# Modulation products of a two-block transformer kernel: fp32 in four column groups, most of them placed in the first block's attentions

## What is computed

```python
mod = (silu_c @ lp["w_mod"] + lp["b_mod"])[:, None, :]
sh1, sc1, gt1, sh2, sc2, gt2 = jnp.split(mod, 6, axis=-1)
h = modulate(x, lp["g_norm1"], sh1, sc1)      # rms_norm(x, g) * (1 + sc1) + sh1
x = x + gt1 * merge_branches(...)
x = x + gt2 * conv_ffn(modulate(x, lp["g_norm2"], sh2, sc2), lp)
```

## Time and profile before

| | |
|---|---|
| median of 3 runs | 2862.47 us (2861.6 to 2864.29) |
| profiled execution | 2865.59 us, span 2863.8 us |
| PE busy | 2627.9 us, 92% of the span |
| DVE, ACT, POOL busy | 61%, 51%, 21% |
| DMA | 450.55 MB, mean 157 GB/s |
| issues of `raw<-in_w_mod` | 192 of 256 KB |

### The profile page before, as it was taken

How to read it: one execution, slowest core, us unless ns; L and a number is a source line. 1 busy time by engine, 2 the same in 40 slices (tenths; PEclk the granted TensorE clock), 3 DMA queues, 4 the chain that set the end, 5 groups by cost and what they waited for, 6 DMA issues and landing times.

```text
span 2863.8 us, 48110 instructions
## 1 busy us (share of the span) xinstructions
PE 2627.9 (92%) x17790; PEld 2304.9 (80%) x17790; DVE 1748.5 (61%) x2491; ACT 1465.8 (51%) x2248; POOL 604.5 (21%) x432
## 2 busy tenths in 40 slices
PE   5769999999899999699999999999799999979998
PEld 2538978988877898588589979978699789857996
DVE  6564756776675776657667756553566554455455
ACT  5454554665445575354446645444454454446444
POOL 0001202332111233221032323212032033011311
PEclk9788999999999999899999999999899999999999
DMA  9684515655541565354135565656156546633663
GB/s 302 207 273 129 164 53 149 182 177 163 156 127 39 154 190 181 92 160 148 38 120 169 182 191 178 195 166 194 48 155 202 172 149 191 187 114 89 191 194 123
DMA packets 332946, 450.55 MB, mean 157 GB/s; under 512 B 28192, under 2 KB 207392, under 8 KB 332768
## 3 DMA queue, kind: packets, MB, share of 16 engines
q1 hardware_dynamic: 332400, 446.58, 50.4%
q0 software_dynamic: 368, 1.57, 0.2%
HBM read 446.99 MB, written 1.05 MB: 156 GB/s over the span
## 4 chain that ended last, share of the span: by engine, by line
PE 82%; DVE 7%; DMA 4%; ACT 4%; issue 2%; POOL 1%; SPq 1%; DVEq 0%; ACTq 0%; POOLq 0%
PE S L818 26%; PE S L809 21%; PE G L818 14%; PE G L809 9%; DMA raw<-in_w_mod 4%; PE TB L868 3%; PE S L897 2%; DVE wlo L603 2%; ACT whi L598 2%; PE G L935 1%; ACT pp L1191 1%; PE TB L776 1%; PE G L920 1%; PE S L959 1%; PE G L959 1%
## 5 line engine op out<-in xcount | busy, mean ns | idle before, releaser
L603 DVE TENSOR_TENSOR wlo<-raw,whi 128x1024 fp32r<-128x1024 f32 x723 | 946.4, 1318 | 779.0 <-ACT whi L598 773.2
L598 ACT CAST whi<-raw 128x1024 fp32r<-128x1024 f32 x872 | 904.5, 1049 | 838.5 <-PE S L809 261.6
L818 PE MATMUL S<-hhi,whi 128*128 128x256 f32 x1952 | 547.6, 281 | 4.0 <-issue 2.4
L818 PE MATMUL S<-hhi,wlo 128*128 128x256 f32 x1952 | 547.7, 281 | 0.0
L818 PE MATMUL S<-hlo,whi 128*128 128x256 f32 x1952 | 546.6, 280 | 0.0
L603 POOL TENSOR_TENSOR wlo<-raw,whi 128x1024 fp32r<-128x1024 f32 x149 | 362.1, 2430 | 758.6 <-ACT whi L598 757.9
L818 PEld LDWEIGHTS S<-hhi,whi 128*128 128x128 f32 x1952 | 367.3, 188 | 5.6 <-issue 5.1
L818 PEld LDWEIGHTS S<-hlo,whi 128*128 128x128 f32 x1952 | 368.6, 189 | 0.2
L818 PEld LDWEIGHTS S<-hhi,wlo 128*128 128x128 f32 x1952 | 368.0, 189 | 0.0
L818 PE MATMUL G<-hhi,whi 128*128 128x256 f32 x1088 | 305.3, 281 | 2.9 <-issue 2.7
L818 PE MATMUL G<-hhi,wlo 128*128 128x256 f32 x1088 | 305.0, 280 | 0.0
(11 more groups left out here) (340 smaller groups left out, 4543.1 us busy)
## 6 DMA issues: line engine op xcount, KB each, us to landing
raw<-in_ffn_wi SPq DMA_DIRECT2D x352, 256.0 KB, 3.5
raw<-in_w_up SPq DMA_DIRECT2D x264, 256.0 KB, 3.5
raw<-in_w_mod SPq DMA_DIRECT2D x192, 256.0 KB, 3.8
raw<-in_w_in SPq DMA_DIRECT2D x192, 256.0 KB, 3.2
raw<-in_ffn_wo SPq DMA_DIRECT2D x160, 256.0 KB, 3.4
raw<-in_w_down SPq DMA_DIRECT2D x120, 256.0 KB, 3.4
raw<-in_a_wqkv SPq DMA_DIRECT2D x72, 256.0 KB, 2.9
raw<-in_w_o SPq DMA_DIRECT2D x48, 256.0 KB, 3.2
```

What stands on the lines that cost most here:

```text
L598: act.copy(whi[:, n0 % SPLIT], raw[:, n0 % RAW]).then_inc(hi_done, 1)
L603: eng.tensor_tensor(wlo[:, n0 % SPLIT], raw[:, n0 % RAW], whi[:, n0 % SPLIT].bitcast(F32), ALU.subtract)\
L818: mm = pe.matmul(out_[:, m * T:(m + 1) * T], w, x, start=first and c == 0 and m == 0 and z == 0, stop=last and c == kc - 1 and z == len(te ...
```

## The change

The stages `mod` and `modcols` of both layers go. One stage `mod` with four units (shift 1 and scale 1 of layer 0) stands at the start. The other 20 units stand inside the first block's attentions: 8 in A (layer 0, pieces 4 to 11), 4 in B (layer 1, pieces 0 to 3), 8 in C (layer 1, pieces 4 to 11), at the steps of the table `MODS`. There is no split: the weights are loaded as fp32 into `modw`, two buffers of a whole unit (2 MB each, 8 DMAs of 256 KB), which lie over `whi` and `wlo`. A unit is 8 matmuls of 512 columns (2 chunks x 4 column groups of 32), all into the bank `G0[1]`; `silz` holds 30 columns of zeros and then the two rows, and its window moves by two columns a unit, so each unit's result comes to rows of its own. One copy (DVE), four small matmuls with `fold` and one addition give all columns of a stage.

Since `G0[1]` is taken, the pairs of these attentions all use `G0[0]`, and their copy and multiplication move to the head of the even steps. Since `modw` covers `whi` and `wlo`, the last unit of `gates` splits nothing ahead; the three slots of `br` are split at the end of the attention instead. SP loads the first four raw slots of `br` before the units, waits until `gates` is multiplied, and then loads the units, each when the one two before it is used. At the start SP loads two units, then the constants and the context, then the other two, then the latents.

```diff
+MODS = {(0, CTX): (0, 4, 8, (0, 1, 4, 8, 11, 14, 17, 19)), (0, LAT): (1, 0, 4, (0, 2, 4, 6)),
+        (1, LAT): (1, 4, 8, (0, 2, 4, 6, 8, 10, 12, 14))}
+MOD_SLOTS, MOD_W = 4, 32
...
-    for l in range(DEPTH):
-        gemm("mod", 6 * D // SN, KD, l=l)
-        add("modcols", u=1, x=1, l=l)
+    add("mod", u=1, mod=(0, 0, 4, ()))
...
+        def value_bank(st, p):
+            return G0[0] if st.mod else G0[p % 2]
+        def lead_steps(st, n):
+            return (n + 1, n + 2, n + 3) if max(st.mod[3]) < n else (n + 4,) * LEAD
...
+            def load_mod(st, i):
+                g = mod_base[st] + i
+                wait_count(sp, mod_used, g - 1)
+                src = mod_source(st, i)
+                for z in range(MOD_SLOTS):
+                    for c in range(SK):
+                        sp.dma_start(modw[:, g % 2 * MOD_SLOTS + z, c, :], src[:, z * SK + c, :]).then_inc(mod_full[g % 2], 16)
...
+                if st.kind == "attn" and st.mod:
+                    ahead = STAGES[STAGES.index(st) + 2]
+                    for k in range(RAW // len(slot_shapes(ahead.kc))):
+                        load_unit(ahead, k, k, 0)
+                    sp.wait_ge(bank_done[1], st.n)
+                    for i in range(st.mod[2]):
+                        load_mod(st, i)
...
+            def mod_unit(st, i):
+                g = mod_base[st] + i
+                pe.wait_ge(mod_full[g % 2], 16 * MOD_SLOTS * SK * (g // 2 + 1))
+                for c in range(SK):
+                    for z in range(MOD_SLOTS):
+                        mm = pe.matmul(G0[1][z * MOD_W:(z + 1) * MOD_W - 2 * i, :], silz[:, z * SK + c, 2 * i:MOD_W],
+                                       modw[:, g % 2 * MOD_SLOTS + z, c, :], start=i == 0 and c == 0,
+                                       stop=i == st.mod[2] - 1 and c == SK - 1, skip_group_check=True)
+                mm.then_inc(mod_used, 1)
+            def mod_fold(st):
+                pe.wait_ge(mod_copied, mods.index(st) + 1)
...
                 for s in range(n + VALUE_LAG):
                     if s < n:
                         scores(s)
                     if TURN_LAG <= s < n + TURN_LAG:
                         turn(s - TURN_LAG)
+                    if st.mod and s in st.mod[3]:
+                        mod_unit(st, st.mod[3].index(s))
                     if s >= VALUE_LAG:
                         values(s - VALUE_LAG)
+                if st.mod:
+                    mod_fold(st)
...
+                        if st.mod and s >= VALUE_LAG + 2 and s % 2 == 0:
+                            weighted((s - VALUE_LAG - 2) // 2)
...
+                        if st.mod and s == n + VALUE_LAG - 1:
+                            mod_copy(st)
+                        if st.mod:
+                            for h in [h for h, step_ in enumerate(lead_steps(st, n)) if step_ == s]:
+                                lo_part(dve, st.n + h, st.n + h, None, None)
+                    if st.mod:
+                        mod_columns(st, 1 + st.pad)
+                        dve.wait_ge(mod_done, mods.index(st) + 1)
+                    dve.wait_ge(pair_free, pair0 + len(pairs_))
+                    dve.tensor_copy(mx[:, 0:1], mhalf[:, 0:1]).then_inc(bank_free[0], 1 + st.pad)
```

More of the change, by code:

```diff
@@ L257, in loop_shape @@
     per = len(slot_shapes(st.kc))
-    if st.kind not in ("mod", "gates", "up", "qkv") or st.units < 2 * PAIRS:
+    if st.kind not in ("gates", "up", "qkv") or st.units < 2 * PAIRS:
         return 0, 0, st.units
@@ L550, in modulation, with mod_source, mods_needed, follows_mod @@
             return amul[:, st.l, w, c, st.s:st.s + 1], modT[:, st.l, 3 * w * KD + c, st.s:st.s + 1]
+        mods = [st for st in STAGES if st.mod]
+        mod_base = {st: sum(z.mod[2] for z in mods[:n]) for n, st in enumerate(mods)}
+        def mod_source(st, i):
+            l, first, count, _ = st.mod
+            c0 = (first + count - 1 - i) * SN
+            return dram["w_mod"][l].rearrange("(c p) n -> p c n", p=P)[:, :, c0:c0 + SN]
+        def mods_needed(st):
+            return 2 * st.l + int(st.which)
+        def follows_mod(st):
+            return st.kind == "gates" and st.part == 1
+        def value_bank(st, p):
+            return G0[0] if st.mod else G0[p % 2]
+        def lead_steps(st, n):
+            return (n + 1, n + 2, n + 3) if max(st.mod[3]) < n else (n + 4,) * LEAD
         def lo_by_pool(st, n0):
@@ L765, in _ @@
         def _(pe):
+            def mod_unit(st, i):
[9 more added lines that the diff above has]
+                pe.wait_ge(mod_copied, mods.index(st) + 1)
+                n = 2 * st.mod[2]
+                for q in range(SN // P):
+                    mm = pe.matmul(G0[1][:, q * n:(q + 1) * n], modsum[:, q * P:(q + 1) * P], fold[:, MOD_W // 2 - n:],
+                                   start=True, stop=True, skip_group_check=True)
+                mm.then_inc(mod_folded, 1)
             def turn_rows(st, n):
@@ L1098, in _ @@
             act.wait_ge(ld_cols, 16)
-            act.activation(silc[:, :, :], col("c", 0, 2 * KD).rearrange("p (k s) -> p k s", s=2), ACT.Silu).then_inc(silc_done, 1)
-            act.wait_ge(silc_done, 1)
-            act.copy(silr[:, :, 0:2], silc[:, :, :]).then_inc(silc_done, 1)
+            act.activation(silz[:, :, MOD_W - 2:], col("c", 0, 2 * KD).rearrange("p (k s) -> p k s", s=2), ACT.Silu)\
+               .then_inc(silz_done, 1)
+            act.wait_ge(ld_ctx, 16)
+            for t in range(NT):
+                row_squares(norms[0], t)
+            act.wait_ge(mod_used, mods[0].mod[2])
             for n in range(LEAD):
@@ L1117, in _ @@
                 if st.kind == "norm" and not inside(st):
-                    if st.which == "1":
+                    if st.which == "1" and st is not norms[0]:
                         for t in range(NT):
```

256 lines of the change are left out of this document (142 added, 114 removed).

## The result

The changed kernel took 2711.89 us in the median of 4 runs (2710.83 to 2713.81), the kernel before 2862.63 (2861.6 to 2864.29) on the same chip: ratio 0.9474, 95% interval 0.9462 to 0.9486. It is faster by 5.3%, as forecast; the forecast of 2702 us was 9.9 us too low. The profiled execution of after took 2710.83 us (span 2709.0), so against the profiled 2865.59 of before the change is worth -154.8 us where the sum said -160.7. The other 4.0 us of the miss are the two executions: before's lies 3.0 over its median, after's 1.1 under.

A forecast was written before the change was run, and what follows sets the result against it. PE was busy 92% of the span, but DMA limited the modulation stage. Start -198.3, A +18.4, B +5.0, C +13.7, rest +0.5 sum to -160.7: 2704.9 from the profiled 2865.6, 2702 us against the median; range 2688 to 2717, to 2740 with rivals.

The forecast's parts named there:

- Start: Kernel start: first chunk of `in` split at 40.6 us instead of 238.9, saving 198.3 us.
- A unit is 1.9 us: PE, each unit: eight matmuls with four column groups at once, 1.72 us plus 0.2 for filling and draining.
- Rivals 1, 2 and 4: Units: two groups at once, about 2735 (chance 0.13); no overlap, 2812 (0.05); no overlap and low clock, 2930 (0.02).
- Loads in A: A's later units land 7.4 us after the unit two before is used; steps take 8 to 9, so no PE wait.
- the 2 us in all: Sign that loads are hidden: PE's waits for DMA into `modw` under 2 us altogether in A, B and C.
- One bank and the place of the product: Attentions: PE waits for the single value bank, costing 2.3 us in A, 1.0 in B, 0.5 in C.
- splits and slack: Ends of B and C: splits within the last steps cost 1.0 us in B, splits and fold 1.5 in C.
- Steps of 3.3 us leave slack: B: its step length was the reason to put the single bank's cost at only 1.0 us.
- Clock: Heads of B and C: a unit in the gap keeps PE's clock up, -3.2 us in B, -1.6 in C.
- End of A: A's end: late splitting puts `br` 7.0 us after the last unit, 2.8 us more from the last values.
- Rest: Other stages: second block's attentions get only other semaphores and two tiny copies, 0.5 us.
- the 25 to 60: A, B and C together: growth under 25 or over 60 us would make the prediction wrong.

The follow-up runs named there:

- later rounding: Changed kernel with ACT rounding a pair's sums after the next even step's exponentials and copy, not at the end of the odd step: 2715.7 us.
- maximum first: Changed kernel with DVE taking the maximum of an even step before it multiplies the pair, not after: 2714.8 us.
- early table: Changed kernel with A's eight units at steps 0, 1, 5, 7, 9, 11, 13, 15 instead of 0, 1, 4, 8, 11, 14, 17, 19: 2711.0 us.

## Why the prediction was right, and where its sizes were off

**Start: -198.3 forecast, -198.8 measured to the first split chunk.** Errors cancel. The units after the norm ran at full clock, 3.7 us in place of 6.8; but the turns ended 2 us later than I had them (30.3, not 28.3), and copy, fold and additions took 2.4 us, not 1.8. So DVE's first low part began at 36.5, forecast 36.9, and three of them took the 3.7 us forecast. The third slot of `in` landed at 37.8 only, since SP asks for it after all four units (390 GB/s over the stretch); it was rounded at 38.90, when DVE had just come free (38.87), so it cost nothing yet, but it would have if anything before it had been faster. The first product follows 1.5 us behind the chunk, before 3.0, which gives the -200.3.

**A unit is 1.9 us: right.** The chain of after in A has its units one by one:

```profile
197.94 1.92 PE G L840 x16
...
209.26 1.85 PE G L840 x16
...
218.10 1.84 PE G L840 x16
```

Rivals 1, 2 and 4 fell with this. Four starts 0.43 us apart, four instructions in each, are 1.72 us and a tail: four at once without loss. The Trainium skill (TensorE: Matmul & The Clock Gate, "Measured speedup vs the span model") has 3.07 for four groups of rows and 2.38 for three of columns; this trace shows the full 4 for four groups of columns, and the measurement decides. Units and their copies together cost 12.5 + 6.0 + 10.6 = 29.1 us where the terms were 13.3 + 6.2 + 13.8 or so: C's were better covered by gaps than I took them.

**Loads in A: "so PE does not wait" failed, by 2.2 us once**, just over the 2 us in all that the prediction had named as its sign. Unit 2 was asked for at 188.43, when unit 0 was used, and landed at 197.94: 9.5 us, not 7.4. The stream of two units ran at 321 GB/s from 190 to 198, not at 401. I had taken the latency from a transfer of 0.29 MB and the rate from another stretch. (The 292 GB/s named as the limit of the old stage was its steady rate, too: over the whole 216 us it was 236, with two `modcols` of 20.6 us in between. The forecast doesn't use it.)

**One bank and the place of the product: under-sized.** "0.6 us at five even steps, 2.3 us" for A, 1.0 for B, 0.5 for C; the runs show 4.1, 1.2 and 1.5 for the bank, and 2.0, 3.1 and 3.0 for what I called splits and slack. "Steps of 3.3 us leave slack" is the sentence that failed. PE has slack there; the circle ACT, DVE, ACT hasn't, and I counted the product's wait for the bank on PE, but not that the next maximum stands behind the product on DVE and the next exponentials behind that. The later rounding shows this circle in B (-1.1 us); maximum first only moved the wait from one member of it to another.

**Clock: right.** -3.2 and -1.6 forecast, -3.4 and -1.7 by the low-clock time of before, and none in after.

**End of A: right.** Forecast 7.0 us from the end of the last unit to `br`, measured 6.9 (240.60 to 247.53). From the last values it is 6.1 where it was 3.4, so 2.75 more for a forecast of 2.8; the fold (0.9) runs within it and before `four2`, which is why the table has only 5.20. With the early table it is 3.35 again behind `four2`, so this end belongs to the late unit.

**Rest: 0.5 forecast, 4.7 measured.** "The second block's attentions only get other semaphores" was true and beside the point. The up products lost 2.1 to 2.3 us each (the first 0.8), the products of `br` 0.5 to 1.9, and most of those of 512 columns won 1.3 to 2.5, because the operands moved in SBUF. No step of the prediction looked at addresses. That isn't the whole sum: two stretches of 512-column products in the second block, at 2354.8 and 2669.2 in after, are 1.5 and 1.7 us longer with the clock at its lower level, and behind C such stretches make 98 us in after's trace and 79 in before's. How much of the 4.7 is the clock was not separated.

Sum of the misses against -160.7: start -2.0, A +2.1, B +1.9, C -0.3, rest +4.2: -154.8. The time fell so close to the forecast partly by luck: the start won 2 us that no step had, and the bank and the place of the product, some 9 us over their terms in the three attentions, were half covered by units and copies 4 us under theirs. All three stages together grew by 40.8, inside the 25 to 60 named beforehand.

## What to carry to other kernels

A DMA-bound stage can be hidden in a stage where PE works and the queue is empty, even at a price on PE: 216 us of loading for 41 us of attentions. Price the order on every engine in such a move, not only on the one that bounds: here the added cost sat in a circle through ACT and DVE. And when a change moves buffers in SBUF, compare the pace of untouched stages before and after: count matmuls per 100 us; 192 unused bytes were worth 34 to 36 us, all the scheduling tried after the change some 4 in stage lengths, and nothing that a time shows.

## What the runs showed of the hardware that was not expected

- The pace of back-to-back 128 x 128 x 256 products depends on where their two operands lie: 120 ns at an offset of 0 bytes modulo 2048, 118 at 1600 and at 416, 113 in most up products at 192, worth 28.7 us in the kernel before (2861.5 to 2832.8) and 34 to 36 us in the changed one (2711.9 or 2714 to 2678.3). Only four remainders were tried, so the period of 2048 is one that fits, not one that was shown: a product takes its weights at steps of 512 bytes and its moving chunks at steps of 1024, so the remainders modulo 512 (0, 64, 416 and 192) fit as well. The Trainium skill (SBUF — State Buffer, "SBUF: two separate sides") says that PE never waits on anyone at SBUF; these runs show that its pace isn't free of placement, and not whom it would wait for.
- The same layout can run a stage at 113 or 118 ns in one execution. In the kernel before the products of `br` do it too: 118.4 ns behind A, 114.0 behind B and C.
- The order in which matmuls of different column groups are issued didn't matter: a unit takes 1.9 us also when the matmuls of one group follow each other in the code.
- At 43.70 us in after a DVE subtraction of two SBUF operands took 2.52 us where its neighbours take 0.43, beside POOL's split from 43.56 to 45.95. The Trainium skill (SBUF — State Buffer, "SBUF: two separate sides") describes a port that such a pair shares and that the one which starts first holds for its whole instruction, and the row agrees with it.
